# Latent attention taken two heads at a time: shared blocks, rope scores in fp32r, scaling on ScalarE

## What is computed

```python
cq  = rms_norm(h_all @ w_dq, g_q)                 # 512 tokens x 384
q   = (cq @ w_uq).reshape(B, T, 8, 128 + 64)      # 128 plain, 64 rope
ckv = h_all @ w_dkv                               # 256 latent + 64 rope key, one for all heads
kv  = (rms_norm(ckv[..., :256], g_kv) @ w_ukv).reshape(B, T, 8, 128 + 128)
q_rope, k_rope = rotated for the latent tokens only
s = q_nope @ k_nope.T + q_rope @ k_rope.T
p = softmax(s * 192 ** -0.5);  o = p @ v
```

## Time and profile before

| | before |
|---|---|
| median of three runs | 1961.38 us (1961.01 to 1962.88) |
| the profiled execution, first to last instruction | 1959.2 us |
| TensorE busy | 1919.3 us (98%) |
| VectorE busy | 1400.5 us (71%) |
| ScalarE busy | 895.7 us (46%) |
| GpSimd busy | 250.2 us (13%) |
| the attention loop of the first layer | about 72 to 228 us |

### The profile page before, as it was taken

The page is one execution under the profiler, slowest core; times in us unless marked ns, Lnnn a source line. Parts: engine busy times, 40 slices in busy tenths (PEclk is TensorE's granted clock), DMA queues, the critical chain, the costliest instruction groups (busy, mean ns, idle before and its releaser), DMA issues.

```text
span 1959.2 us, 27475 instructions
## 1 busy us (share of the span) xinstructions
PE 1919.3 (98%) x10285; PEld 1607.6 (82%) x10285; DVE 1400.5 (71%) x2243; ACT 895.7 (46%) x1536; POOL 250.2 (13%) x332
## 2 busy tenths in 40 slices
PE   8999999999999999999999999999999999989998
PEld 4877788888888777889988888888888878878997
DVE  5898777888866655487997676767755567667765
ACT  3433355333343453576554224634233454557654
POOL 2101010211111200411101001101110021331000
PEclk9999999999999999999999999999999999999999
DMA  8434235655663451367875422655555245327763
GB/s 311 138 98 136 76 98 185 211 184 174 201 185 100 158 168 33 95 225 257 271 245 165 151 97 69 200 162 183 161 172 161 78 148 176 98 92 229 228 196 116
DMA packets 191827, 315.12 MB, mean 161 GB/s; under 512 B 14637, under 2 KB 114312, under 8 KB 191696
## 3 DMA queue, kind: packets, MB, share of 16 engines
q1 hardware_dynamic: 162512, 210.09, 33.0%
q0 software_dynamic: 29184, 103.29, 17.1%
HBM read 312.29 MB, written 1.05 MB: 160 GB/s over the span
## 4 chain that ended last, share of the span: by engine, by line
PE 82%; DVE 9%; issue 4%; ACT 2%; DMA 2%; POOL 1%; SPq 0%; DVEq 0%; POOLq 0%; ACTq 0%
PE bank L723 24%; PE bank L730 22%; PE bank L729 22%; PE bank L733 8%; DVE w L2242 3%; DVE acc L2267 2%; PE bank L728 2%; PE bank L726 2%; ACT junk L1642 1%; PE bank L785 1%; DMA raw<-in_mlp_w 1%; POOL st L3258 1%; PE bank L809 1%; DVE X L2386 1%; ACT w L1610 1%
## 5 line engine op out<-in xcount | busy, mean ns | idle before, releaser
L1610 ACT ACTIVATE w<-raw 128x1024 fp32r<-128x1024 f32 (+4 forms) x390 | 399.1, 1031 | 555.8 <-PE bank L730 481.8
L2242 DVE TENSOR_TENSOR w<-raw,w 128x1024 fp32r<-128x1024 f32 (+3 forms) x372 | 439.2, 1189 | 229.2 <-ACT w L1610 228.8
L723 PE MATMUL bank<-HH,w 128*128 128x256 f32 (+1 forms) x1552 | 509.5, 328 | 3.4 <-DVE HH L2369 2.0
L729 PE MATMUL bank<-HL,w 128*128 128x512 f32 (+1 forms) x1232 | 412.1, 334 | 0.0
L730 PE MATMUL bank<-HH,w 128*128 128x512 f32 (+1 forms) x1232 | 411.9, 334 | 0.0
L2267 DVE SCALAR_TENSOR_TENSOR acc<-ada,sc,acc 128x512 f32<-128x512 f32 x518 | 362.4, 746 | 2.3
L723 PEld LDWEIGHTS bank<-HH,w 128*128 128x128 f32 x1552 | 291.0, 188 | 30.5 <-issue 4.4
L723 PE MATMUL bank<-w,UH 128*128 128x512 f32 x768 | 300.7, 392 | 0.3 <-DVE UL L2544 0.3
L730 PE MATMUL bank<-w,UL 128*128 128x512 f32 x768 | 299.1, 390 | 0.0
L729 PE MATMUL bank<-w,UH 128*128 128x512 f32 x768 | 298.9, 389 | 0.0
L729 PEld LDWEIGHTS bank<-HL,w 128*128 128x128 f32 x1232 | 230.2, 187 | 26.1 <-issue 0.2
(11 more groups left out here) (354 smaller groups left out, 2610.1 us busy)
## 6 DMA issues: line engine op xcount, KB each, us to landing
raw<-in_mlp_w SPq DMA_DIRECT2D x256, 512.0 KB, 4.4
ada<-in_mod_w POOLq DMA_DIRECT2D x96, 512.0 KB, 4.5
ada<-in_ada_w POOLq DMA_DIRECT2D x80, 512.0 KB, 4.7
raw<-in_ml_w_qkvo SPq DMA_DIRECT2D x28, 512.0 KB, 3.7
raw<-in_conv_w_in SPq DMA_DIRECT2D x24, 512.0 KB, 4.2
raw<-in_ada_w SPq DMA_DIRECT2D x12, 512.0 KB, 6.1
raw<-in_mla_w_o SPq DMA_DIRECT2D x8, 512.0 KB, 3.9
raw<-in_gla_w_v SPq DMA_DIRECT2D x8, 512.0 KB, 4.0
```

Source lines behind the costliest of these rows:

```text
L723: pe.matmul(o, sh, mh, start=start, stop=False, skip_group_check=True)
L729: pe.matmul(o, sh, ml, start=False, stop=False, skip_group_check=True)
L1610: act.activation(k.halves(n)[0], k.raw[(NDIRECT + n) % NRAW][:, 0:m], ACT.Copy).then_inc(*k.w_hi.up("w hi", n))
L2242: dve.tensor_tensor(low, k.raw[(NDIRECT + n) % NRAW][:, 0:m], high.bitcast(F32), ALU.subtract).then_inc(*k.w_lo.up("w lo", n))
```

## The change

- The up-projection weights come as three blocks for two heads in place of four: `first` (head 2p's 128 plain query columns, the 64 rope columns of head 2p, and those of head 2p+1), `both` (keys and values of both heads, 1,024 columns of buffer), `second` (head 2p+1's plain query columns). `first` is loaded as two transfers.
- The rope queries of two heads come out of one block of nine products, 64 rows each, and are rotated together. The values of two heads come out of products over 256 columns.
- The rope part of a score is no longer one fp32 product over a half empty operand: the high and the low half of the rope queries are stacked on 128 rows (`QR`), and two fp32r products with the stacked key (`KRH` twice the high part, `KRL` twice the low part) give all four partial products.
- The factor 192 ** -0.5 goes into the copy of the queries; the maxima are negated by the reduction itself; the two context tiles share one score bank and one maximum instruction; the reciprocals are taken two at a time.
- The probabilities are scaled by ScalarE instead of VectorE, after the exponentials and before the output's high part; ScalarE also copies both context tiles of the transposed weights.
- During the loop the low parts of the weight blocks are taken by GpSimd.
- The stage has 28 blocks in place of 32, with a rate of 1.45 in place of 1.2.
- Buffers are laid out anew and three memsets are gone.

```diff
-    for name, h in [("q", 0), ("q", 1), ("kv", 0), ("kv", 1)] + [(name, h) for h in range(2, 8) for name in ("q", "kv")]:
-        c = 192 if name == "q" else 256
-        yield wide(A["mla_w_u" + name][0][:, h * c:(h + 1) * c].rearrange("(k p) n -> p k n", p=128))
+    WQ = A["mla_w_uq"][0].rearrange("(k p) n -> p k n", p=128)
+    WKV = A["mla_w_ukv"][0].rearrange("(k p) n -> p k n", p=128)
+    for p in range(4):
+        c = p * 384
+        first = (WQ[:, :, c:c + 192], WQ[:, :, c + 320:c + 384])
+        both = WKV[:, :, p * 512:(p + 1) * 512]
+        second = WQ[:, :, c + 192:c + 320]
+        for block in (first, both, second) if p else (first, second, both):
+            yield wide(block)
...
-LENGTH = [(32, 64), (33, 64), (32, 64), (37, 64)]
-RATE = [(1.2, 1.05), (0.65, 0.45), (0.4, 0.8), (0.8, 0.35)]
+LENGTH = [(28, 64), (33, 64), (32, 64), (37, 64)]
+RATE = [(1.45, 1.05), (0.65, 0.45), (0.4, 0.8), (0.8, 0.35)]
...
+        def first_queries(p):
+
             n = walk.take()
             wh, wl = block_ready(n)
+            from_queries(("qr", p), wh, wl, 128)
+            block_used_with(n, from_queries(("qn", 2 * p), wh, wl, 0))
+
+        def second_queries(p):
+            n = walk.take()
+            wh, wl = block_ready(n)
+            block_used_with(n, from_queries(("qn", 2 * p + 1), wh, wl, 0))
+
+        both = {}
...
+        def pair_values(p):
+            n = both[p]
+            wv = [x.rearrange("p q (h n) -> p q h n", h=2)[:, :, :, 128:256] for x in block_ready(n)]
+            bs = [ps.take("v", p, j) for j in range(2)]
             for t in range(4):
+                b = bs[t // 2]
+                w.wait_ge(*b.before())
+                o = b[:, t % 2 * 256:t % 2 * 256 + 256].rearrange("p (h n) -> p h n", h=2)
                 for q in range(2):
-                    p = mm3(b[:, t * 128:t * 128 + 128],
-                            (k.CKH[:, q, t * 128:t * 128 + 128], k.CKL[:, q, t * 128:t * 128 + 128]),
-                            (wh[:, q, 128:256], wl[:, q, 128:256]), q == 0, q == 1)
-            p.then_inc(*b.filled())
-            block_used_with(n, b)
-            ps.give(b)
-            rope(h, k.qr[h % 2][0:64, :], ps.of("qr", h).is_empty())
+                    m = mm3(o, (k.CKH[:, q, t * 128:t * 128 + 128], k.CKL[:, q, t * 128:t * 128 + 128]),
+                            (wv[0][:, q], wv[1][:, q]), q == 0, q == 1)
+                if t % 2:
+                    m.then_inc(*b.filled())
+            block_used_with(n, bs[1])
+            ps.give(*bs)
...
+            def score(o, c, nk):
+                mm(o, k.qn[i][:, c:c + 128], k.kn[i][:, 0:nk], True, False)
+                mm(o, k.QR[i][:, c:c + 128], k.KRH[:, 0:nk], False, False)
+                return mm(o, k.QR[i][:, c:c + 128], k.KRL[:, 0:nk], False, True)
+
+            for t in range(2):
+                b = ps.take("s", h, 1, t)
+                w.wait_ge(*b.before())
+                score(b[:, :], 256 + t * 128, 512).then_inc(*b.filled())
+                ps.give(b)
...
         for h in range(9):
-            if 0 < h < 7:
-                queries(h + 1)
-            if h < 7:
+            if h % 2 and h < 7:
+                first_queries((h + 1) // 2)
                 keys(h + 1)
+                rope_queries((h + 1) // 2)
+            elif h % 2 == 0 and h < 8:
+                if h:
+                    second_queries(h // 2)
+                keys(h + 1)
+                pair_values(h // 2)
             if h > 0:
                 weights(h - 1)
             if h < 8:
...
+        def rope_high(p, i):
+            r = i * 64
+            w.wait_ge(*at("roped", p))
+            if p:
+                w.wait_ge(*ps.of("s", 2 * p - 2 + i, 0).full())
+            act.activation(k.QR[i][r:r + 64, :], k.qx[r:r + 64, :], ACT.Copy).then_inc(*k.rope_hi.up("rope hi", p, i))
...
+            for half, P, j in ((1, k.Pl, 0), (0, k.Pc, 2)):
+                w.wait_ge(*at("p recip", h, half))
+                w.wait_ge(*ps.of("s", h, 0).is_empty())
                 for t in range(2):
-                    b = ps.of("s", h, half, t)
-                    st = k.st_p[:, i, half * 2 + t, :]
-                    w.wait_ge(*at("score max", h, half, t))
-                    if h >= 2:
-                        w.wait_ge(*ps.of("pT", h - 2, half, t).full())
-                    act.activation(P[2 * i + t][:, 0:nk], b[:, 0:nk], ACT.Exp, bias=st[:, 1:2], scale=192.0 ** -0.5,
-                                   accum_out=st[:, 2:3]).then_inc(*b.emptied())
+                    p = P[2 * i + t][:]
+                    act.activation(p, p, ACT.Copy, scale=rec[:, j + t:j + t + 1]).then_inc(*k.p_scaled.up("p scaled", h, half, t))
...
+        keys_rope_high()
+        walk.take()
         keys(0)
+        rope_high(0, 0)
+        walk.low_by_pool = True
         for h in range(9):
-            if 0 < h < 7:
+            if h % 2 and h < 7:
+                walk.take()
+                rope_queries((h + 1) // 2)
                 queries(h + 1)
-            if h < 7:
+                walk.take()
+                keys(h + 1)
+            elif h % 2 == 0 and h < 8:
+                if h:
+                    walk.take()
+                    queries(h + 1)
+                rope_high(h // 2, 1)
                 keys(h + 1)
             if h > 0:
                 weights(h - 1)
+            if h % 2 and h < 7:
+                rope_high((h + 1) // 2, 0)
             if h < 8:
                 scores(h)
             if h > 0:
                 values(h - 1)
+        walk.low_by_pool = False
...
         for f in (5, 3, 4):
             turned(f)
-        queries(0)
-        rope("k", k.krT[0:64, :])
+        rope("k", k.kx, 64)
         walk.take()
-        queries(1)
-        keys(0)
+        walk.take()
+        w.wait_ge(*ps.of("qr", 0).is_empty())
+        rope(0, k.qx, 128)
+        keys_rope_low()
+        walk.take()
+        rope_low(0, 0)
+        walk.low_by_pool = True
         for h in range(9):
-            if 0 < h < 7:
-                queries(h + 1)
-            if h < 7:
-                keys(h + 1)
+            if h % 2 and h < 7:
+                walk.take()
+                walk.take()
+                rope((h + 1) // 2, k.qx, 128)
+            elif h % 2 == 0 and h < 8:
+                if h:
+                    walk.take()
+                rope_low(h // 2, 1)
+                pair_values(h // 2)
             if h > 0:
                 weights(h - 1)
+            if h % 2 and h < 7:
+                rope_low((h + 1) // 2, 0)
             if h < 8:
                 scores(h)
             if h > 0:
                 values(h - 1)
+        walk.low_by_pool = False
...
-        takes(16)
+        takes(3)
+        walk.low_by_pool = True
+        takes(9)
+        walk.low_by_pool = False
```

More of the change, by code:

```diff
@@ L669, in cap, with pieces @@
         return self.A["consts"][:, a:a + n]
+    def pieces(self, n):
+        b = self.blocks[n]
+        if isinstance(b, tuple):
+            return list(b)
+        return [b[:, :, i, :] for i in range(b.shape[2])] if len(b.shape) == 4 else [b]
     def size(self, n):
-        s = self.blocks[n].shape
-        return s[1], math.prod(s[2:])
+        p = self.pieces(n)
+        return p[0].shape[1], sum(x.shape[2] for x in p)
     def halves(self, n):
@@ L1094, in scores @@
             w.wait_ge(*ps.of("kn", h).is_empty())
-            w.wait_ge(*at("roped", h))
-            w.wait_ge(*at("roped", "k"))
-            w.wait_ge(*at("rope rows"))
-            for half, nk in ((1, 512), (0, 256)):
-                for t in range(2):
-                    c = half * 256 + t * 128
-                    b = ps.take("s", h, half, t)
-                    w.wait_ge(*b.before())
-                    mm(b[:, 0:nk], k.qn[i][:, c:c + 128], k.kn[i][:, 0:nk], True, False)
-                    mm(b[:, 0:nk], k.qr[i][:, c:c + 128], k.krT[:, 0:nk], False, True).then_inc(*b.filled())
-                    ps.give(b)
+            w.wait_ge(*at("rope lo", h // 2, i))
@@ new lines, in scores @@
+            w.wait_ge(*at("rope lo", "k", 0))
+            def score(o, c, nk):
[4 more added lines that the diff above has]
+                b = ps.take("s", h, 1, t)
+                w.wait_ge(*b.before())
+                score(b[:, :], 256 + t * 128, 512).then_inc(*b.filled())
+                ps.give(b)
@@ L1119, in values @@
+            b = ps.take("pT", h, 0)
+            w.wait_ge(*b.before())
+            for t in range(2):
+                w.wait_ge(*at("p scaled", h, 0, t))
+                for kt in range(2):
+                    c = kt * 256 + t * 128
+                    p = pe.transpose(b[:, c:c + 128], k.Pc[2 * i + t][:, kt * 128:kt * 128 + 128], k.ident[:])
+            p.then_inc(*b.filled())
+            ps.give(b)
         def values(h):
+            V = k.VV[h // 2 % 2][:, :, h % 2 * 128:h % 2 * 128 + 128]
@@ L2622, in scores, with pair_values @@
+        def pair_values(p):
+            for j in range(2):
```

(15 more changed lines are left out.)

244 lines of the change are left out of this document (130 added, 114 removed).

## The result

The changed kernel takes 1971.76 us (median of 4 runs, 1970.39 to 1972.94); the kernel before, on the same chip, 1961.2 us. The ratio is 1.0053, interval 1.0041 to 1.0064: 10.6 us slower. The profiled execution's span is 1968.6 us against 1959.2. The prediction said 1963.5 us and a range of 1943 to 1971. One execution of the kernel before (5548.39 us, beside e5 to e8) and one of e13 (2760.58 us) were in a slow state and are left out of every median and ratio here.

A forecast was written before the change was run, and what follows sets the result against it. TensorE, 98% busy, was taken as the bound, with VectorE right behind. Removed 30, waits 23 to 30 and clock 4 to 7 us gave +2 on 1959.2, plus 2.2 from span to median: 1963.5 us, range 1943 to 1971.

The forecast's parts named there:

- The likeliest case: Whole kernel: removed work nearly all returns as waiting and half clock; 1963.5 us, own range 1957 to 1970, chance 0.50.
- The waits: Attention loop: TensorE waits 28 to 35 us against some 5 before, so 23 to 30 come back.
- VectorE is freed of 9 us: Attention loop: nine low halves, 7,680 columns, go to GpSimd from block 15 on, relieving VectorE of 9 us.
- The clock: Behind TensorE's long stops: half clock at 1.94 us for each of five stops, taken as 4 to 7 us net.
- The time outside the loop: Ahead of and behind the head loop: no change; a move of over 3 us would mean a missing term.
- Work removed: TensorE in the attention loop: rope queries, values, rope scores and rope product lose 30.7 us together, taken as 30.
- Rival 4: Values and rope scores: 256-column fp32r products do not reach 0.115 us; alone 1968 us, chance 0.04.
- The stops: TensorE stops before the first scores, at values of heads 0, 2 and 4, in head 6, at banks and tail.
- The load waits: VectorE waits for modulation loads queued behind GpSimd's splits: 6.5 us in head 1, 3 each in heads 3 and 5.
- Rival 3: Heads 3, 5 and 6: GpSimd's splits hold up accumulations, four clashes of 1.7 us, 6.8 slower; 1970 us, chance 0.15.
- Rival 1: Heads 1, 3 and 5: modulation loads are not late, 18 us faster than the main forecast; 1945 us, chance 0.26.
- The scaling: ScalarE takes four scalings per head, 2.0 us, and has room, though they precede the output's high part.

The follow-up runs named there:

- e5: Changed kernel with the first stage's rate of background units back at 1.2 instead of 1.45: 1984.95 us, ratio 1.0118 to the kernel before.
- e8: Changed kernel with the four scalings of a head's probabilities back on VectorE: 1966.11 us, ratio 1.0028 to the kernel before.
- e13: Kernel before with only the loads of the background units issued two units ahead: 1962.73 us, ratio 1.0004 to the kernel before.
- e1: Changed kernel with GpSimd issuing each modulation load two units ahead, across chunk boundaries: 1966.88 us, ratio 1.0025 to the kernel before.
- e6: Changed kernel with loads two units ahead across chunks and a rate of 1.2 background units: 1971.5 us, ratio 1.0055 to the kernel before.
- e4: Changed kernel with unused identity transposes keeping TensorE busy in four stops, against half clock: 1969.27 us, ratio 1.0040 to the kernel before.
- e7: Kernel before with only the low halves from block 15 on given to GpSimd: 1980.01 us, ratio 1.0097 to the kernel before.
- e9: Changed kernel with loads two units ahead, rate 1.2 in the heads and 2.0 in four output projection blocks: 1964.32 us, ratio 1.0018.
- e10: Changed kernel with loads two units ahead, rate 1.3 in the heads and 1.6 in four output projection blocks: 1964.28 us, ratio 1.0020.

## Why the prediction was wrong

The likeliest case had TensorE's work at -30, waits at +26.5 and the clock at +5.5. Measured: -29.3, +29.3, +7.3, and +2.1 outside the loop. Each moved the same way: 0.7 + 2.8 + 1.8 + 2.1 = 7.4 us, and the median stood 3.2 us above the span instead of 2.2, since the profiled execution was the fastest of the four. That is 1963.5 to 1971.9. TensorE's stops, their places and most of their sizes were right; why VectorE was late was right only in part.

The steps of the sum that failed are three. The waits were put at +26.5 and measured +29.3: they rest on "VectorE is freed of 9 us", while the splits that freed it took 12.5 us back, and 1.1 of the 2.8 is the 5 us taken for the kernel before, which has 3.9. The clock was put at +5.5 and measured +7.3. The time outside the loop was put at nothing, without a reason, and measured +2.1.

- **Work removed.** Right: 29.3 against 30. Fp32r products over 256 columns start 0.12 us apart (87.11, 87.23, ...), against the 0.115 taken. Rival 4 falls. The layouts had a slip: they gave TensorE's head 14.0 and 14.2 us, but 18.4 less an eighth of 30.7 is 14.5, and the pairs of heads from 123.44 to 162.19 and from 162.19 to 201.48, stops and half clock taken off, come to 14.9 and 14.8 a head.
- **The stops.** Predicted before the first scores 6, measured 5.55; at the values of head 0 7.3 to 8.3, measured 9.47; at those of heads 2 and 4 4 to 6, measured 5.49 and 5.87; head 6 3 to 5, measured 0.31 + 0.82 + 0.86; bank waits and tail 4, measured 1.23 + 0.99 + 1.22 + 1.41. The sum of 33.2 lies inside the 28 to 35. I took the middle, and it came near the top. Head 0's 9.47 lies over its own range by 1.2 or more, and the addition stretched to 2.25 us stands ahead of it; head 6's lies under its range.
- **The load waits.** Head 1: 6.5 predicted, 6.68 measured. Heads 3 and 5: 3 each predicted, 1.42 and 0.26 measured. That the stops of heads 3 and 5 fell into their range is luck: VectorE was late by 4.9 and 5.1 us, of which the stretched instructions beside the splits were 3.5 and 4.8. In all, 12.5 us of load waits were predicted and no clash; measured are 8.4 and 12.5. Rival 3 had the place and the price of a clash (1.7 us; 1.3 to 2.7 measured each) but counted it as an addition to the load waits. In heads 3 and 5 it largely replaced them, so it did not come to 6.8 us on top. The Trainium skill (SBUF — State Buffer, "Who interferes with whom") has such a VectorE instruction wait out the whole of GpSimd's; the trace agrees, down to an instruction on 128x4 elements that took 2.25 us, though which of the two came first is not always to be seen (last section).
- **Rival 1** (loads not late, 18 us faster) is what e1 tested: 4.9 us, not 18. Its condition was met and its price was wrong, because the clashes were behind the waits and the lump behind both (e6). Its chance of 0.26 was thus put on a case that could not reach its time.
- **The scaling.** "ScalarE has room for the sum" was right and beside the point: e8 shows some 5 us for its order ahead of HH. They took ScalarE 0.72 us for 512 columns and 0.49 for 256, 2.4 a head against the 2.0 taken. In my layout HL comes at 4.8 with the scalings ahead of it, but I compared that with no layout without them.
- **The clock.** 4 to 7 predicted, 7.3 measured, from 9.0 less 1.7. Five long stops at 1.94 us each were counted; there were four, at 2.25 in the mean. The deduction for stretches where VectorE is late anyway has the right size by e4, which wins only 4.2 of the 9.0 in the loop, but the measured waits came out no lower for it.
- **Outside the loop.** 2.1 us, under the 3 that were to tell of a missing term: behind the loop 1.0 less; ahead of it 3.1 more, of which 1.7 is a stretch at half clock and 0.7 a stop at 75.16 for VectorE that the kernel before does not have. At 44 to 52 us, after and before:

```profile
44.00:52.00 8.00, 7.68 (x43) 7.44 (x43) 5.93 (x14) 5.36 (x11) 0.00 (x0) 0.79 0.50 145
```

```profile
44.00:52.00 8.00, 7.68 (x50) 7.34 (x50) 6.34 (x14) 5.79 (x11) 0.00 (x0) 1.00 0.42 137
```

The stretch is at 1.00 in the kernel before, e4, e7 and e9, and at 0.79 in the changed kernel and the ten others, e13 among them; what decides it is open.

## What to carry to other kernels

A subtraction moved from VectorE to GpSimd is not free for VectorE: look for every VectorE instruction that can fall beside it (here those that read two SBUF tensors, the tiny ones too, and in e1 one that reads a single one), and for what else stands in GpSimd's queue behind it. When a change shortens the work of the engine that was the bound, lay out the order of the engine that is next with and without each moved piece, up to the next point where all must be done, since time won in a loop can be lost as a lump behind it. Where two causes of lateness stand one behind the other, undoing one uncovers the other: price them together.

## What the runs showed of the hardware

- A VectorE addition on 128x4 elements takes 0.16 us alone. Beside a split of GpSimd it took up to 2.82 us, and its end fell within 0.04 us of the split's end: 194.11 and 194.08 in head 5, 153.85 and 153.83 in head 3, 109.64 and 109.62 in e1. In head 5 its record begins 0.41 us ahead of the split's, so the order of the two starts doesn't settle who waits.
- Behind a stop of 1.4 us at 235.96 the twelve products took 2.83 us, the time at full clock, behind those of 5.5 us and more 4.5 to 5.3. In between, the length of the stop does not decide it: in e10 the same twelve took 2.83 us behind a stop of 2.84 (115.01) and 4.35 behind one of 2.83 (150.33), and the granted clock stayed at 1.00 behind the first and was 0.50 at 152 to 154 us behind the second.
- At 46 to 50 us, with the same work of TensorE, a stretch at half clock came in eleven of the fifteen kernels and stayed away in four, worth some 1.7 us: a difference of that size between two single profiles may be no more than this.
